# Routing the first head pair of a stretch before or after the residual that closes the one before it

## What is computed

```python
def peer_ffn(h, wq, k1, k2, u, v):          # 8 heads, 128 keys a side, top 16 of 16 x 16
    q = (t @ wq)...reshape(n_tok, PEER_HEADS, 2, PEER_HALF)
    s1, s2 = q[:, :, 0] @ k1.T, q[:, :, 1] @ k2.T
    v1, i1 = lax.top_k(s1, PEER_TOPK)
    v2, i2 = lax.top_k(s2, PEER_TOPK)
    cand = v1[..., :, None] + v2[..., None, :]
    sc, pos = lax.top_k(cand, PEER_TOPK)
    gate = softmax(sc)
    ue = u[idx]                              # one row of 1024 floats for each token, head and choice
    act = gate * gelu(dot(token, ue))
    y = sum(act * v[idx])
x = x + gt2 * y
```

## Time and profile before

| | us |
|---|---|
| median of 3 runs | 2222.76 (2215.66 to 2250.27) |
| the profiled execution | 2223.44 |
| its span | 2221.6 |
| PE busy | 1550.8 (70%) |
| DVE busy | 1258.0 (57%) |
| POOL busy | 1183.2 (53%) |
| ACT busy | 290.8 (13%) |

### The profile page before, as it was taken

One profiled execution on the slowest core, in us unless ns is written; L12 is line 12 of the kernel. 1 busy time (PEld: TensorE's weight loads), 2 busy tenths in 40 slices (PEclk: granted clock), 3 DMA queues, 4 the chain that ended last, 5 costly groups with the idle time before them and its releaser, 6 DMA issues.

```text
span 2221.6 us, 20587 instructions
## 1 busy us (share of the span) xinstructions
PE 1550.8 (70%) x7636; PEld 911.2 (41%) x7636; DVE 1258.0 (57%) x2811; ACT 290.8 (13%) x589; POOL 1183.2 (53%) x1063
## 2 busy tenths in 40 slices
PE   6978884867976738768778364786878830656666
PEld 2634672433422636546555163555655500100011
DVE  3353476655542888797330598778743049646440
ACT  0021110000001231221111132022121100000000
POOL 0000057676655466676654346466665336777774
PEclk9988996686688869889989786998989975777669
DMA  8550499999999968988999596797799858999997
GB/s 349 216 204 10 159 380 360 411 412 411 412 390 335 346 217 293 368 301 287 411 401 358 197 362 216 260 362 298 279 401 413 329 192 295 364 355 365 368 369 265
DMA packets 174293, 706.45 MB, mean 318 GB/s; under 512 B 24033, under 2 KB 24417, under 8 KB 156785
## 3 DMA queue, kind: packets, MB, share of 16 engines
q0 software_dynamic: 147456, 536.94, 64.7%
q1 hardware_dynamic: 26736, 168.19, 19.0%
HBM read 704.00 MB, written 1.05 MB: 317 GB/s over the span
## 4 chain that ended last, share of the span: by engine, by line
POOL 22%; DVE 20%; DMA 18%; PE 16%; issue 11%; ACT 2%; another core or an unknown queue 1%; POOLq 0%; ACTq 0%; DVEq 0%
DMA vb<-in_peer_v,idx 13%; POOL vb L1877 12%; POOL ub L1868 10%; DVE ub L1083 6%; PE PS L1529 5%; DMA ub<-in_peer_u,idx 4%; PE PS L1562 2%; DVE ring L1211 1%; DVE ring L1156 1%; DVE ring L1204 1%; DVE ring L1157 1%; DVE ring L1137 1%; PE PS L1835 1%; PE PS L1708 1%
## 5 line engine op out<-in xcount | busy, mean ns | idle before, releaser
L1083 DVE CUSTOM_DVE_ANT_0 ub<-ub,h 128x1024 f32<-128x1024 f32 x512 | 628.4, 1238 | 413.3 <-DMA ub<-in_peer_u,idx 376.2
L1877 POOL DMA_INDIRECT vb<-in_peer_v,idx x512 | 561.6, 1097 | 396.3 <-PE PS L1529 244.2
L1868 POOL DMA_INDIRECT ub<-in_peer_u,idx x512 | 569.6, 1113 | 334.9 <-issue 134.5
L1529 PE MATMUL PS<-vb,z 128*32 128x512 f32 x2048 | 564.1, 758 | 228.0 <-DMA vb<-in_peer_v,idx 211.9
L1529 PEld LDWEIGHTS PS<-vb,z 128*32 128x32 f32 x2048 | 92.3, 122 | 624.7 <-DMA vb<-in_peer_v,idx 464.5
L1625 PEld LDWEIGHTS PS<-hT,ring 128*128 128x128 f32 x1024 | 124.5, 202 | 17.2 <-issue 14.7
L1625 PE MATMUL PS<-hT,ring 128*128 128x128 f32 x1024 | 127.5, 287 | 3.7 <-DMA ring<-in_gdn_qkv 1.8
L1854 POOL IOTA iota<- 128x16 f32 x1 | 0.1, 149 | 240.7 <-POOLq L407 240.7
L1072 DVE TENSOR_TENSOR h<-PS,mods 128x1024 f32<-128x1024 f32 x4 | 4.9, 1225 | 201.4 <-PE PS L1494 201.4
L1583 PEld LDWEIGHTS PS<-c_act,ring 128*128 128x128 f32 x512 | 77.5, 242 | 23.3 <-issue 23.2
L278 PE MATMUL PS<-ring,hT 128*128 128x512 f32 x192 | 83.3, 593 | 0.7 <-ACT hT L467 0.7
(11 more groups left out here) (295 smaller groups left out, 2055.1 us busy)
## 6 DMA issues: line engine op xcount, KB each, us to landing
ring<-in_gdn_qkv SPq DMA_DIRECT2D x32, 1024.0 KB
ring<-in_ada_late SPq DMA_DIRECT2D x28, 1024.0 KB
ring<-in_peer_wq SPq DMA_DIRECT2D x24, 1024.0 KB
ring<-in_ada_w SPq DMA_DIRECT2D x10, 2048.0 KB, 8.3
ring<-in_gdn_z SPq DMA_DIRECT2D x16, 1024.0 KB
ring<-in_gdn_w_out SPq DMA_DIRECT2D x16, 1024.0 KB
ring<-in_gla_w_in SPq DMA_DIRECT2D x6, 2048.0 KB, 11.9
ub<-in_peer_u,idx POOLq DMA_INDIRECT x512
```

The source lines that it names most:

```text
L1083: dve.tensor_tensor_reduce(out=ub[:, n % UB, :], in0=ub[:, n % UB, :], in1=h[:, t, :], scale=1.0, scalar=0.0, op0=ALU.mult, op1=ALU.add, a ...
L1529: last = pe.matmul(y[32 * j:32 * j + 32, e, :], z[:, j, 28 * b:28 * b + 32], vb[:, n % VB, e * 512:(e + 1) * 512], start=False, stop=False ...
L1868: pool.indirect_dma_start(ub[:, n % UB, :], None, u_rows, off).then_inc(u_land[n % UB].sem, 16)
L1877: pool.indirect_dma_start(vb[:, n % VB, :], None, v_rows, off).then_inc(v_land[n % VB].sem, 16)
```

## The change

`routing` and `softmax` of pairs 8 and 12 (the first pairs of stretches 2 and 3) move into the closing part of the stretch ahead. There they get a due time `ROUTE_AT` (461 after the start of that stretch), which lies behind `weights(k - 1)` and ahead of the residual. ACT's `exp` of these pairs gets a due time to match. No instruction is added or taken away, and the lists of PE, ACT, POOL and SP come out in the same order as before.

```diff
+            ROUTE_AT = {w: W_AT[w - 1] + 461.0 for w in (2, 3)}
...
-                                if p == 0 and w != 1:
-                                    yield t0 - 42 if w == 0 else t0 + 1.5
+                                if p == w == 0:
+                                    yield t0 - 42
                                     for i, _ in enumerate(routing(k)):
-                                        yield t0 - 40 + 2 * i if w == 0 else t0 + 1.5
+                                        yield t0 - 40 + 2 * i
                                     softmax(k)
                                 if p == PAIRS:
                                     yield t0 + 1
                                     weights(k - 1)
+                                    if w + 1 in ROUTE_AT:
+                                        yield ROUTE_AT[w + 1]
+                                        for i, _ in enumerate(routing(k)):
+                                            yield ROUTE_AT[w + 1] + 2 * i + 2
+                                        softmax(k)
                                     yield t0 + span + 1
...
-                                if p == 0 and w != 1:
-                                    yield t0 - 20 if w == 0 else t0 + 1.5
+                                if p == w == 0:
+                                    yield t0 - 20
                                     exp(k)
...
+                                if p == PAIRS and w + 1 in ROUTE_AT:
+                                    yield ROUTE_AT[w + 1] + 21
+                                    exp(k)
```

## The result

| | before | after |
|---|---|---|
| median on the same chip | 2233.82 (2215.66 to 2255.92, 11 runs) | 2197.11 (2186.02 to 2213.74, 11 runs) |
| the profiled execution | 2223.44 | 2201.55 |
| its span | 2221.6 | 2199.8 |

The ratio is 0.9848, with a 95% interval of 0.9820 to 0.9876. The change makes the kernel about 34 us faster (by the ratio; the medians differ by 36.7), where 43.8 us had been worked out. The time lies inside the range of 2166 to 2198 us by less than 1 us. Part of the miss in the time itself is the base: the kernel before took 2233.82 us here, 11 us more than the 2222.76 that the forecast stood on.

A forecast was written before the change was run, and what follows sets the result against it. No single engine was taken to bound the kernel; behind each residual the core waits for routing. 21.25 + 19.92 + 2.6 = 43.8 us off 2223.4 gave 2179.6 us, range 2166 to 2198.

The forecast's parts named there:

- seam 1, residual to `norm_inv`: Between stretches 1 and 2: the token mixer's chain starts 21.25 us earlier once the routing no longer follows the residual.
- seam 2, residual to `idx` of pair 13: Before stretch 3: first dot 19.92 us earlier, plus 2.6 us of DVE's gather wait gone in the first pair.
- The cover of the wait: Ahead of both residuals: `softmax` waiting for ACT's `exp` costs nothing, with 37 and 34 us to spare.
- The rival in which this wait reaches the residual: Late score copies make `softmax` delay residual, mixer and dots; 2267 us if `exp` comes 80 us later; chance 0.02.
- Does the rest of stretch 2 keep it?: Stretch 2 behind seam 1 slides as a whole; loss taken as 0, bounded by 0 to 21 us.
- The rival in which a seam gives nothing: Stretch 2 has another floor, such as weight loads, and gives back its 21.25 us: 2201 us; chance 0.10.
- POOL's whole lead: Rival: gathers set the pace and each seam gives the 26.9 us POOL gains: 2169.6 us; chance 0.13.
- the first cost: Closing parts: `v` gathers slowed beside DVE's routing, at most 4.2 us a seam, taken as 0.
- The second cost: End of closing parts: early `u` gathers delay landing `v` gathers; taken as 0, bounds -0.4 and +19 us a seam.
- The rival of this cost: Early `u` gathers hold up the last `v` gathers, 6 us or so a seam: 2192 us; chance 0.10.
- A measurement of this kernel can tell about 2% from no change: Whole kernel: edge at 2178.3 against 2222.76 us; the forecast's 0.65 split 0.30 below, 0.35 above; within 2% got 0.55.
- at 1242 and about 1782: Predicted residual starts at seams 1 and 2; the forecast is wrong if the second moved by less than 18 us.

The follow-up runs named there:

- g: Comparison with kernel before at 2231.73 us: the changed kernel run again took 2197.01 us, ratio 0.9878.
- h: Comparison with kernel before at 2253.47 us: the changed kernel took 2222.28 us, ratio 0.9899; each routing was also moved alone.
- k: Comparison with kernel before at 2241.97 us: the changed kernel, ratio 0.9808, and the changed kernel with early `u` gathers held, ratio 0.9863.
- e_uheld: Changed kernel, but POOL waits for the residual before the first `u` gather of pairs 8 and 12, fastest chip: 2156.29 us, ratio 0.9846 against before.
- k_uheld: Changed kernel with POOL held until the residual before the first `u` gather of pairs 8 and 12, slower chip: 2211.5 us, ratio 0.9863 against before.
- k_after: Changed kernel, unedited, run beside the one with `u` gathers held: 2201.53 us, ratio 0.9808 against before at 2241.97 us.
- h_after: Changed kernel, unedited, run a fourth time: 2222.28 us, ratio 0.9899 against before at 2253.47 us, interval 0.9785 to 1.0014.
- h_seam1: Only the routing of pair 8 moved, against the kernel before, second time: 2237.33 us, ratio 0.9938.
- e_again: Changed kernel, unedited, run a second time on the fastest chip: 2145.82 us, ratio 0.9803 against before at 2187.82 us.

## Why the prediction was right and wrong

**The place of the gain: right.** The terms of the sum, against what the traces have:

| term | worked out | fastest chip | the other chips |
|---|---|---|---|
| seam 1, residual to `norm_inv` | 21.25 | 21.2 | 21.2 |
| seam 2, residual to `idx` of pair 13 | 19.92 + 2.6 = 22.5 | 23.1 | 23.1 |
| what it costs in the closing parts | 0 | 0 | 9.4 |
| sum | 43.8 | 44.3 | 34.9 |
| ratio times the time before | | 43 | 34 (first), 27 (g), 23 (h), 43 (k) |

The 34.9 lies near the 34 of the first comparison, but the four comparisons spread from 23 to 43, so that agreement is partly luck, and the 9.4 rests on the traces alone. Seam 0 was a good model for seams 1 and 2: the 1.14 us to the first dot, the 4.58 to `norm_inv` and the 1.24 to the first `u` gather came out to a tenth of a microsecond.

**The cover of the wait: right.** `softmax` waited 14.02 us, and DVE was idle for 42.4 us behind it. The rival in which this wait reaches the residual never came near.

**"Does the rest of stretch 2 keep it?": right, as far as it can be told.** With pair 8 alone moved 18.5 us (medians) to 24 us (ratio) come out at the end of the program on the fastest chip, with an interval of 16 to 31. The traces agree more loosely: from residual 1 to the next closing part are 504.6 us on the mean of the three slower traces without the move and 485.5 on the five with it, 19 us less, and on the fastest chip 482.9 against 470.9 and 469.3. The rival in which a seam gives nothing is out, and so is the one of POOL's whole lead: that would have been 54 us. e_uheld shows what POOL's lead is worth, some 10 us of the 43 (10.0 again in k_uheld against k_after, where four runs a side tell little).

**"What it costs": wrong, in its size and its reason.** I took 0 for both costs. In the slower comparisons the traces have 9.4 us for them together, for which the sum of 43.8 holds nothing. The bound of the first cost, 4.2 us a seam, was of the right size, but by a mechanism that isn't there: the gathers beside the routing take 0.93 to 1.17 us on POOL, about as before, and the 1.99 us of the earlier trace rows doesn't occur there. What lengthens the closing part is the hand-over from PE to ACT and to DVE, which stood nowhere in my list of costs. I had PE down as the engine that is waited for, with nothing that could slow it. Why the hand-over is late stays open.

The second cost, `v` rows held up by early `u` gathers, was looked for in the landing times, and there it isn't. PE's last `v` matmuls in the changed kernel start 6.55 us after the last `v` gather is sent (1249.60):

```profile
1256.15 1.90 PE L1538 MATMUL PS<-vb,z 128*32 128x512 f32 x10 [0.23 <-issue]
```

In the kernel before they start 6.50 us after it (1231.80):

```profile
1238.30 1.90 PE L1529 MATMUL PS<-vb,z 128*32 128x512 f32 x10 [0.17 <-DMA vb<-in_peer_v,idx]
```

The 3.5 us stand behind them, between the closing sums and the residual. The rival of this cost has a slip of its own: half of the price of a gather in a crowd, which is 19 us by the same text, is 9.4 us a seam and not 6, so that its time should have been 2198 and not 2192.

**"A measurement of this kernel can tell about 2% from no change": wrong.** Eleven runs a side give an interval of 0.28% to each side. So 34 us, or 1.5%, is a clear gain, and even the 1.1% of a single seam is. This is the step that made the most likely answer "within 2%" out of a forecast of 1.97% less, when the same sum put no chance but 0.02 on the other side. All forecasts from 2166 to 2201 us were forecasts of a faster kernel.

**The residuals "at 1242 and about 1782": wrong by 21 and 23 us**, and by my own test the second had to move by 18 us, and moved 2.5 the other way. Of the first 21 us, 9.0 are the closing part, 8.5 stand ahead of the residual of seam 0 and 3.8 in the untouched part of stretch 1 (468 us before, 472 after, 459 to 481 over the traces). Seam 2 adds 4.0 in its closing part. The test asked two executions to agree at one point in time, which they don't to 10 us, while the two distances of the first table (residual to `norm_inv` and to `idx`) are steady to 0.1 us over the traces of the changed kernel and its halves where the routing has moved, and to 0.4 us where it hasn't.

## What to carry to other kernels

Work out a move between two events of the same seam and check it there: the distance from residual to `norm_inv` read 5.8 us in every trace of the changed kernel and of pair 8 alone, while the median of the kernel before moved by 66 us from comparison to comparison. An engine that was idle while others worked is free time, but filling it can still slow the others: compare the filled stretch with the unfilled one in the same trace, which moving only one of two like pieces gives for nothing. And before a forecast is cut by what a measurement can tell, take that from the spread and the number of runs.

## What the runs showed of the hardware

- One and the same kernel took 2187.82, 2231.73, 2233.82, 2241.97 and 2253.47 us in five comparisons. The fastest was on a chip whose traces hold all but 3 to 15 of the 16384 records of the gathers' semaphores.
- In the four others ACT can start 2.3 us after PE's last matmul has ended in the records. In h_after PE then stands still for 2.6 us, and its granted clock falls from 2.4 to 1.2 GHz, where 8 matmuls of 128 columns take 2.08 us instead of 1.16 (h_seam1).
- A gather issued by POOL takes a slot of 1.24 us in its row (0.94 + 0.30) while DVE is idle. In four traces (before, after, e_again, k_after) the 989 gathers with no DVE instruction beside them took at most 0.99 us, and those beside dots up to 1.99. Eight of them put among the `v` gathers lengthen the closing part by 10 us, even where POOL had waited 9.72 us for a buffer just before; whether by POOL's row or by the DMA engines, which were busy for 1.01 of the time, isn't told apart.
